# A transformer kernel with an expert gather: a quarter of one block's V rows given to ScalarE and GpSimd, and the routing of later heads interleaved with the first dots

## The reference, cut to what matters

```python
s1 = einsum('thd,nd->thn', q[..., :half], keys_1); s2 = einsum('thd,nd->thn', q[..., half:], keys_2)
v1, i1 = top_k(s1, 16); v2, i2 = top_k(s2, 16)
cand = (v1[..., :, None] + v2[..., None, :]).reshape(t, 8, 256)
sc, ci = top_k(cand, 16)
experts = e1 * 128 + e2                      # 8 heads x 16 = 128 experts for each token
gates = softmax(sc)
a = gelu(einsum('td,ted->te', h, u_tab[experts]))
out = einsum('te,ted->td', gates * a, v_tab[experts])
```

## Time and profile before

| what | value |
|---|---|
| median of 3 runs | 2451.01 us (2449.72 to 2452.77) |
| the profiled execution: its time / its span | 2452.18 us / 2449.7 us |
| busy: PE, PEld, DVE, ACT, POOL | 83%, 52%, 61%, 40%, 38% |
| mean granted TensorE clock | 0.928 |
| bytes moved by DMA | 726.56 MB, 540.59 MB of it on the queue of the gather |

### The profile page before, as it was taken

How to read it: one execution, slowest core, us unless ns; L and a number is a source line. 1 busy time by engine, 2 the same in 40 slices (tenths; PEclk the granted TensorE clock), 3 DMA queues, 4 the chain that set the end, 5 groups by cost and what they waited for, 6 DMA issues and landing times. The chain is left out here.

```text
span 2449.7 us, 22093 instructions
## 1 busy us (share of the span) xinstructions
PE 2045.3 (83%) x7187; PEld 1270.5 (52%) x7187; DVE 1504.8 (61%) x2990; ACT 991.0 (40%) x2299; POOL 920.8 (38%) x681
## 2 busy tenths in 40 slices
PE   6997867897898776777799888879999968687999
PEld 3775645553454222232465334446666547456787
DVE  5748446678886677755678876766777732442111
ACT  3206443424333222222444577444343334344443
POOL 3522002233444334343223444333343326004887
PEclk9987678899999999999899999989999989798999
DMA  7720035799999999999899999999999934002554
GB/s 270 270 89 1 1 137 214 293 421 387 422 415 405 418 421 422 422 420 421 344 391 381 421 367 368 387 361 377 421 421 421 421 145 152 18 1 92 183 189 154
DMA packets 111069, 726.56 MB, mean 297 GB/s; under 512 B 12519, under 2 KB 13546, under 8 KB 29802
## 3 DMA queue, kind: packets, MB, share of 16 engines
q0 software_dynamic: 74800, 540.59, 54.0%
q1 hardware_dynamic: 35520, 184.43, 20.0%
q10 hardware_dynamic: 634, 0.14, 0.0%
HBM read 716.45 MB, written 8.66 MB: 296 GB/s over the span
## 5 line engine op out<-in xcount | busy, mean ns | idle before, releaser
L1350 PE MATMUL ps<-uv_ring_a,expert_diag_a 128*128 128x512 f32 x1920 | 910.6, 619 | 206.1 <-ACT expert_diag_a L1329 187.3
L1121 POOL DMA_INDIRECT uv_ring_a<-in_peer_uv_dram,expert_idx x512 | 581.3, 1135 | 965.4 <-PE ps L1350 927.7
L1270 DVE CUSTOM_DVE_ANT_0 uv_ring_a<-uv_ring_a,x_rows 128x1024 f32<-128x1024 f32 x512 | 620.9, 1220 | 176.6 <-DMA uv_ring_a<-in_peer_uv_dram,expert_idx 174.8
L1350 PEld LDWEIGHTS ps<-uv_ring_a,expert_diag_a 128*128 128x128 f32 x1920 | 365.8, 197 | 669.2 <-issue 364.6
L1314 ACT ACTIVATE expert_gelu_a<-expert_dot_a 128x2 f32<-128x2 f32 x256 | 52.1, 204 | 774.4 <-DVE expert_dot_a L1270 771.8
L1430 POOL TENSOR_TENSOR w_low_b<-w_raw_b,w_high_b 128x1024 fp32r<-128x1024 f32 x98 | 233.6, 2393 | 256.1 <-ACT w_high_b L1422 255.2
L1430 DVE TENSOR_TENSOR w_low_a<-w_raw_a,w_high_a 128x1024 fp32r<-128x1024 f32 x142 | 173.5, 1222 | 188.1 <-ACT w_high_a L1422 186.1
L1422 ACT CAST w_high_a<-w_raw_a 128x1024 fp32r<-128x1024 f32 x146 | 151.2, 1038 | 100.5 <-PE ps L1443 80.0
L1329 ACT ACTIVATE expert_diag_a<-ident,expert_weight_a 128x128 f32<-128x128 f32 x480 | 168.6, 395 | 0.4 <-ACT expert_weight_a L1320 0.4
L1422 ACT CAST w_high_b<-w_raw_b 128x1024 fp32r<-128x1024 f32 x98 | 102.7, 1051 | 121.2 <-PE ps L1443 76.0
L1320 ACT ACTIVATE expert_weight_a<-expert_gelu_a,expert_gate 128x1 f32<-128x1 f32 x512 | 122.8, 287 | 8.9
(11 more groups left out here) (460 smaller groups left out, 3268.1 us busy)
## 6 DMA issues: line engine op xcount, KB each, us to landing
w_raw_a<-in_w_gu_dram SPq DMA_DIRECT2D x22, 1024.0 KB
w_raw_b<-in_w_gu_dram SPq DMA_DIRECT2D x22, 1024.0 KB, 4.9
w_raw_a<-in_w_peer_q_dram SPq DMA_DIRECT2D x16, 1024.0 KB
w_raw_a<-in_w_out_dram SPq DMA_DIRECT2D x12, 1024.0 KB
w_raw_a<-in_w_in_dram SPq DMA_DIRECT2D x12, 1024.0 KB
w_raw_b<-in_w_in_dram SPq DMA_DIRECT2D x12, 1024.0 KB, 4.9
w_raw_a<-in_w_down_dram SPq DMA_DIRECT2D x11, 1024.0 KB
w_raw_b<-in_w_down_dram SPq DMA_DIRECT2D x11, 1024.0 KB, 4.8
```

The lines of the kernel that those rows point to most:

```text
L1121: pool.indirect_dma_start(out=self.ring[:, n % self.RING, :], out_offset=None, in_=K.uv, in_offset=bass.IndirectOffsetOnAxis(ap=K.idx[self ...
L1270: dve.tensor_tensor_reduce(u, u, self.h[b][:, :], 1.0, 0.0, ALU.mult, ALU.add, self.a[:, s:s + 1]).then_inc(self.s_dot, 1)
L1350: ins = nc.tensor.matmul(self.bank(half), self.diag[q % self.DIAGS][:, :], self.ring[:, n % self.RING, D + 512 * half:D + 512 * half + 512 ...
```

## The change

In block 2 every fourth slot (32 slots: n = 259, 263, ... 383) is now taken from PE. ACT scales its V row in place (`Copy` with the weight as scale, 128x1024), and POOL adds the row to expert_sum, in its own stream just ahead of the DMA that reuses the place. The first of them (n = 259) is written by ACT straight into expert_sum. `own` goes from 3 to 2, so that block 2 also ends with the form of `update` that adds expert_sum.

In block 0, group 1 (heads 2 and 3) is begun with 14 steps ahead of the first dot, and its other 24 steps are spread over the dots of slots 0 to 16. Group 2 follows in slots 17 to 46, block 1's two groups in slots 48 to 99. The `exps` and `gates` of groups 0, 1 and 2 move with them, and so do the loads of block 1's scores on SP (from 12 and 36 slots to 20 and 52). ACT also takes tail a's evictions of query group j = 1 for the second token block from DVE.

```diff
@@ class Gather
+    BEGUN = 14
+    POOLED = (2,)
+    PACES = ((0, 17, 24), (17, 47, 68), (48, 100, 138))
...
+            self.s_own, self.s_scaled = K.sem("expert_added_here"), K.sem("expert_scaled")
...
+    def pooled(self, n):
+
+        return n // SLOTS in self.POOLED and self.here(n)
@@ def sp
-                    yield self.at(36 if hg else 12)
+                    yield self.at(52 if hg else 20)
@@ def pool
-            yield self.at(n - self.RING + 2.5)
+            q = n - self.RING
+            if self.pooled(q) and q % SLOTS >= self.share:
+                yield self.at(q + 2.2)
+                pool.wait_ge(self.s_scaled, (q - self.alone) // self.share)
+                pool.wait_ge(self.s_own, (q - self.alone) // self.share)
+                pool.tensor_tensor(self.acc[:, :], self.ring[:, q % self.RING, D:2 * D], self.acc[:, :],
+                                   ALU.add).then_inc(self.s_own, 1)
+            yield self.at(q + 2.5)
@@ def dve
-        for i in range(2):
-            first = self.route(dve, ch, i)
-            for n in range(self.steps(2)):
-                yield tail.scored[i] + 0.25 * n
-                next(first)
-            yield tail.scored[i] + 0.25 * self.steps(2) + 1.5
-            gates(i)
+        first, second = self.route(dve, ch, 0), self.route(dve, ch, 1)
+        for n in range(self.steps(2)):
+            yield tail.scored[0] + 0.25 * n
+            next(first)
+        for n in range(self.BEGUN):
+            yield tail.scored[1] + 0.25 * n
+            next(second)
+        yield tail.scored[1] + 0.25 * self.BEGUN
+        gates(0)
...
-                steps, over, lag = 2 * self.steps(4), 88, 0
+                paces = ((0, 88, 2 * self.steps(4)),)
                 if b == 0:
-                    ahead, steps, over, lag = chain(self.route(dve, ch, 2), ahead), steps + self.steps(4), 92, 10
+                    ahead = chain(second, self.route(dve, ch, 2), ahead)
+                    paces = self.PACES
...
-            while done * over < steps * (s + 1 - lag) and done <= steps:
+            due = sum(steps * min(max(s + 1 - lo, 0), hi - lo) / (hi - lo) for lo, hi, steps in paces)
+            while routing and done < due:
                 next(ahead, None)
                 done += 1
-            if s == 42 and b == 0:
-                gates(2)
+            if b == 0 and s in (21, 51):
+                gates(1 if s == 21 else 2)
...
-                    if self.here(q):
+                    if self.here(q) and not self.pooled(q):
                         add(q)
@@ def act
-        for i in range(2):
-            yield self.tails[0].scored[i] + 0.25 * self.steps(2) + 0.5
-            exps(i)
+        yield self.tails[0].scored[1] - 0.4
+        exps(0)
...
             for n in range(g * G, g * G + G):
+                if self.pooled(n):
+                    v, x = self.ring[:, n % self.RING, D:2 * D], self.w[:, n % SLOTS:n % SLOTS + 1]
+                    act.wait_ge(self.s_w, n + 1)
+                    if n % SLOTS < self.share:
+                        act.wait_ge(self.s_y, 4 * b)
+                        act.activation(self.acc[:, :], v, ACT.Copy, scale=x).then_inc(self.s_own, 1)
+                    else:
+                        act.activation(v, v, ACT.Copy, scale=x).then_inc(self.s_scaled, 1)
                 if self.here(n):
                     continue
...
-            if g == 19:
-                exps(2)
+            if b == 0 and g in (9, 24):
+                exps(1 if g == 9 else 2)
@@ class Tail, def act and def dve
-        yield from self.evict(act, lambda b, j: b == 0 or j >= self.prompt > 0, act.copy)
+        yield from self.evict(act, lambda b, j: b == 0 or j >= self.prompt - 1 > 0, act.copy)
...
-        yield from self.evict(dve, lambda b, j: b == 1 and not j >= self.prompt > 0, dve.tensor_copy)
+        yield from self.evict(dve, lambda b, j: b == 1 and not j >= self.prompt - 1 > 0, dve.tensor_copy)
@@ def stage_first
-        g = Gather(K, c1, list(range(TB)), x, 0.0, 2.6, (6, 7), 8, 4, 3)
+        g = Gather(K, c1, list(range(TB)), x, 0.0, 2.6, (6, 7), 8, 4, 2)
```

More of the change, by code:

```diff
@@ L1031, in __init__ @@
             self.acc = K.sb(ctx, "expert_sum", [P, D])
-            self.s_own = K.sem("expert_added_here")
+            self.s_own, self.s_scaled = K.sem("expert_added_here"), K.sem("expert_scaled")
         self.ring = K.sb(ctx, "uv_ring", [P, RING, 2 * D])
```

## The result

The changed kernel has a median of 2488.91 us (2479.89 to 2490.84, 4 runs) against 2450.36 us (2449.22 to 2452.77, 4 runs) of the kernel before on the same chip. The ratio is 1.0143, 95% interval 1.0124 to 1.0163: about 38 us **slower**. The profiled execution is the fastest of the four, 2479.89 us. Forecast were 2435 us and a gain.

What follows compares the result with a forecast made beforehand. The prediction took the gather as bound by DMA traffic at about 421 GB/s, with only slower stretches to win; -12 - 2 - 6 + 1 + 1 + 1 = -17 us gave 2435 us, range 2412 to 2454 with rivals.

Steps and rivals of the forecast that it cites:

- What DVE gets: +1: Block 2: POOL's additions delay DVE's two-input operations by 38 us, mostly absorbed by DVE's room; +1 us, bounds 0 and +8.
- Rival B: Block 2: every addition blocks DVE for most of 2.4 us, so DVE takes PE's place; 2450 us, no change, chance 0.15.
- Rival C: Block 2: POOL both adds and issues DMAs, so late additions delay DMAs; 2476 us, at a full addition 2514, chance 0.12.
- Block 2: 32 V rows leave PE, -6: Block 2, 1200 to 1340, where PE was 98% busy: half of 12.0 us lost there is won; bounds 0 and -12.
- Rival A: Block 2: PE's relief pays in full, 27.7 us, with no cost on ACT and DVE; 2410 us, chance 0.12.
- Routing spread: -12: Gather's start: ninth DMA at about 440 instead of 451.84, with evictions and exps moved; -12 us, bounds -5 and -21.
- The other 24 steps stand beside idle DVE: nothing: Gather's start: group 1's 24 remaining steps run beside dots where DVE had idled, so they cost nothing.
- SP: -2: Gap at 590 to 606: the later score load no longer holds up tail b's stores and weights; -2 us, bounds 0 and -4.
- Rival D: Gather's start: first gap closes but the next grows, slots 8 to 16 carrying routing; 2445 to 2448 us, chance 0.06.
- ACT +1: Block 2, 1400 to 1520: scalings replacing diagonals add 7.6 us to an ACT 80% busy; +1 us, bounds 0 and +8.
- update +1: End of block 2: `update` has one more 128x512 operation in each half, 0.7 us each; +1 us.
- the other signs: Signs named beforehand: no-traffic stretch gone, first dot before 435, 1200 to 1340 shorter, block 2 dots over 1.22 us, last stage equal.

Runs made afterwards that it cites:

- e5: The changed kernel with POOL writing zeros (two memsets, about as long, no SBUF read) in place of each addition; 2456.74 us, 1.0015 of the kernel before.
- e1: The kernel before with only the start's part of the change, block 2 as before; 2446.63 us, 0.9974 of the kernel before.
- the five: Five executions with the same block 2 instructions: the kernel before, e1, e9 and two other variants of e1; block 2 took 390.8 to 395.5 us.
- e4: The changed kernel with POOL's addition cut to 16 of 1024 columns, waits, order and ACT's scaling kept; 2451.86 us, 1.0006 of the kernel before.
- e11: The changed kernel with POOL's addition on 16 columns and PE given products of the gate rows for the rows that left it; 2453.41 us, 0.999.
- e9: e1 with an even pace of routing for group 2 and block 1 (206 steps in 92 slots); 2440.44 us, 0.9941 of the kernel before.
- e2: The kernel before with only the block 2 part of the change, the start as before; 2484.05 us, 1.0125 of the kernel before.
- e6: e1, every V row on PE, plus 30 unneeded POOL additions of 128x1024 in block 2 at the change's places; 2465.62 us, 1.006 of the kernel before.
- e8: The changed kernel with PE given two products of the gate rows in place of each of 30 pooled rows; 2482.08 us, 1.0134 of the kernel before.

## Why the prediction was wrong, by its own steps

- **"What DVE gets: +1" is the step that failed.** It had the pair of operations from the earlier trace rows and priced an addition at 1.2 us of DVE, 38 us in all. Measured: 51 us, about 1.6 each, so that was nearly right. The path was wrong: the term was put at +1 and turned out as 30 us (changed kernel against e5), because of what it made of the delays: DVE had room, so most would cost nothing. Room in a mean says nothing of a wait within a chain. The dot stands in the round of a ring place (DMA, dot, gelu, diagonal, product, next DMA), and there are only eight places. By the timelines of POOL and DVE, over 120 slots of block 2, the mean from a slot's issue to its dot went from 15.6 us in e1 to 16.9, and from the dot to the issue eight slots on from 9.6 to 10.7. That the round is 2.5 us longer isn't a second proof of the loss: eight slots begin in a round, so 2.5 / 8 x 128 = 39 is the longer block 2 (37.8 us) put in other words. What is new is where the time goes, and e5 shows how much is the port's: with memsets the first part is 15.7 us again and the second 10.0. One late dot delays more than its own place, since the streams of DVE, ACT and PE are in order: slots that aren't pooled are hit too (dot to issue 9.7 to 10.6). So a dot's delay isn't shared out among the eight places. 51 us of delay on DVE became 30 us of block 2, about six tenths, although DVE was idle for a quarter of the time before.
- **Rival B** had this mechanism and the wrong size (2450), for it counted DVE's free time as a cushion as well. It gave the port 7 us in block 2 and took away the 6 of PE's relief; the port alone is 30 (changed kernel against e5).
- **Rival C** had nearly the size (2476 at half an addition a row) with the wrong mechanism. POOL waited 7.6 us for its own additions and 0.6 before them, and queue and dependency cost 8 to 11 us (e5 against e1 or the mean of the five), 0.25 to 0.34 us a row, below the 0.44 from which C would decide. The sign named for it, DMAs released mostly by own additions, isn't there; the fall of traffic, 381 to 347 GB/s, is.
- **"Block 2: 32 V rows leave PE, -6": nothing.** e4 and e11 have no port in the way, the one with and the other without the relief: 397.7 and 398.8 us, both longer than e1. The 12.0 us in the earlier trace rows were read as PE's, since it was 98% busy there. In e4 PE is at 88% in that stretch, traffic is 3 GB/s higher (1 us by the prediction's formula), and ACT waits 58.9 us for dots there instead of 46.0: taking one engine's load away left the rest of the chain as long. The DMA share of 0.98 in that row, which the prediction did name, was the better guide. Rival A falls with it.
- **"Routing spread: -12" was right at the ninth DMA**, 12.3 us earlier in e1, and 2.6 of them from the evictions. The reason is the one given, but the number has luck in it: the weight tile landed 4.0 us earlier after the stage's first load (ACT rounds it at 423.60 in e1, at 430.94 before), where the sum used 0.9, and from there to the ninth DMA it took 12.6 us instead of 10.2. The no-traffic stretch is gone (356 GB/s), the first dot is at 422, before 435 as said.
- **"The other 24 steps stand beside idle DVE: nothing" and "SP: -2"** fell between slots 48 and 128. From a lead of 19.6 us in e1 3.4 remained, and between 1 and 7 in the traces with this pace. The prediction named a start of block 1 not earlier by 10 us as a sign of being wrong, and it was 4.3 us earlier. 8.9 of e1's 16.2 us are new lost traffic, by the sum above; where the other 7 went no run shows. The routing that makes room at the start is paid back by a denser one behind: 138 steps in 52 slots instead of the 206 in 92. With the even pace 11.3 us stay to slot 128 (e9). This pace moves the softmax of group 2 as well, so pace and softmax aren't told apart. SP's later loads weren't tried alone. Rival D had this idea with the gap too early (slots 8 to 16).
- **ACT +1 and update +1** fit e4, 2 to 5 us over block 2 without pooled rows, with POOL's waits in it. The last stage is of equal length, 459 us for 458 from the barrier before it to the end.
- Of the other signs, the longer dots came (a mean of 1.42 us, some near 4), and 1200 to 1340 did not get shorter at over 400 GB/s: it has 349.

The sum as it turned out, against before: start -3, PE 0, ACT, update and hand-over +2, queue +6, port +30: +35. The two traces are 34.7 us apart from the stage's first load on, the medians 38.6. Only the port's term stands far above the 5 us by which equal kernels differ.

The Trainium skill (SBUF — State Buffer, section "Who interferes with whom") names the pair, and says that a GpSimd instruction that only writes doesn't contend with such a DVE instruction. This case agrees: 1216 ns with memsets, 1422 with additions.

## What to carry to other kernels

An addition moved from PE or DVE to GpSimd is not free for VectorE: look first whether VectorE's operations read two SBUF tiles, and whether one of them stands in a latency chain that returns buffers. Take such a delay for lost time in large part (here 30 of 51 us), because it holds every in-order stream behind it; don't subtract it from an engine's idle time, and don't divide it by the number of buffers. A busy engine isn't a bound as long as the rest of the chain is as long: PE went from 98% to 88% and nothing was won. And of a lead that is won at the start of a long stage, follow it to the stage's end: here the same steps at an even pace kept 11 of 12 us, an uneven one 3 (1 to 7 by other traces).

## What was not expected of the hardware

- The dot at 1391.58 started 0.30 us before POOL's addition and still took 3.75 us; that at 1379.63 started 1.36 us after it and took 2.10. Both end 1.1 us after the addition ends (1394.23 and 1395.33; 1380.62 and 1381.73), as if all of the dot's reading came behind it. A dot or w_low that starts earlier still isn't touched; then it is the addition that grows:

```profile
1345.28 1.22 DVE L1287 CUSTOM_DVE_ANT_0 uv_ring_a<-uv_ring_a,x_rows 128x1024 f32<-128x1024 f32 x1
1345.92 2.78 POOL L1128 TENSOR_TENSOR expert_sum_a<-uv_ring_a,expert_sum_a 128x1024 f32<-128x1024 f32 x1
...
1449.04 4.01 DVE L1287 CUSTOM_DVE_ANT_0 uv_ring_a<-uv_ring_a,x_rows 128x1024 f32<-128x1024 f32 x1
1449.60 2.35 POOL L1128 TENSOR_TENSOR expert_sum_a<-uv_ring_a,expert_sum_a 128x1024 f32<-128x1024 f32 x1
```

The line between the two is sharp. In the traces of the changed kernel, e2, e6 and e8 every dot or w_low with a recorded start 0 to 0.57 us before an addition ends 1.1 us after it, 3.1 to 4.0 us long, and each that starts 0.63 us or more before it keeps its 1.2 to 1.3 us. So one of the two is held whole, and the recorded starts decide who, once DVE's is given a handicap of 0.6 us. The pair of the first stage in the earlier trace rows has the same end: 1.1 us after POOL's. The same section of the Trainium skill says that the order of issue decides who blocks, and that the first has the shared ports for the whole instruction. The traces agree if DVE is taken to claim its port some 0.6 us after its recorded start, which is an inference from these rows.
- The price falls on DVE for the most part: 26 of the 31 additions take 2.35 to 2.41 us, and five that begin 0.64 to 0.92 us behind a dot take 2.55 to 2.78. The nearest row of before has 2389 ns.
- PE's granted clock in block 2 went from 0.94 to 0.88 with a tenth less PE work (e1, e4) and to 0.95 when the work was given back (e11), and the time didn't follow it: 395.5, 397.7, 398.8 us.
